# A hybrid decoder layer on one core: column sums of the adaLN projection shared otherwise between PE and DVE, a table's DMAs on another queue, and rows transposed before they are scaled

## The reference

```python
c_act = jax.nn.silu(c)
mod = c_act @ w_ada[l] + b_ada[l]
shift1, scale1, gate1, shift2, scale2, gate2 = jnp.split(mod, 6, axis=-1)

h = modulate(rms_norm(x, norm1_gain[l]), shift1, scale1)      # h * (1 + scale) + shift
proj = h @ w_in[l]
# ... attention with a relative position bias from rel_bias_table[t5_bucket(dist)],
# ... gated linear attention, and their gated merge
x = x + gate1[:, None, :] * (merged @ w_out[l])

h2 = modulate(rms_norm(x, norm2_gain[l]), shift2, scale2)
x = x + gate2[:, None, :] * conv_ffn(h2, w_ffn_up[l], ffn_conv_w[l], ffn_conv_b[l], w_ffn_down[l])
```

## Time and profile before

| | |
|---|---|
| median of 3 runs | 1686.44 us (1682.76 to 1691.81) |
| the profiled execution's own time | 1683.97 us |
| its span in the profile | 1681.8 us |
| PE, DVE, ACT busy | 96%, 71%, 49% of the span |
| PE's granted clock, mean | 0.972 |

### The profile page before, as it was taken

The page is one execution under the profiler, slowest core; times in us unless marked ns, Lnnn a source line. Parts: engine busy times, 40 slices in busy tenths (PEclk is TensorE's granted clock), DMA queues, the critical chain, the costliest instruction groups (busy, mean ns, idle before and its releaser), DMA issues.

```text
span 1681.8 us, 24152 instructions
## 1 busy us (share of the span) xinstructions
PE 1614.8 (96%) x8963; PEld 1400.2 (83%) x8963; DVE 1194.7 (71%) x1312; ACT 818.5 (49%) x971; POOL 30.4 (2%) x36
## 2 busy tenths in 40 slices
PE   4898889999999999999999799999999999999998
PEld 4777889998789988888888688888888888888887
DVE  5777735658877877988886667666666766789553
ACT  5344435346756653443444455555555555433332
POOL 0000000000002200000000000000000000000000
PEclk8888999999989999999999899999999999999999
DMA  7988877766756789998997366666666666799663
GB/s 284 346 294 304 296 178 258 265 233 200 260 166 213 226 281 341 354 342 323 335 329 255 101 189 190 186 194 188 188 188 190 191 190 188 279 376 348 203 206 114
DMA packets 195235, 411.72 MB, mean 245 GB/s; under 512 B 14754, under 2 KB 19406, under 8 KB 194654
## 3 DMA queue, kind: packets, MB, share of 16 engines
q1 hardware_dynamic: 195006, 410.53, 73.9%
q10 hardware_dynamic: 160, 0.26, 0.0%
HBM read 405.23 MB, written 5.25 MB: 244 GB/s over the span
## 4 chain that ended last, share of the span: by engine, by line
PE 91%; DVE 3%; ACT 2%; DMA 2%; issue 1%; SPq 0%; ACTq 0%; DVEq 0%
PE ps L1358 90%; DMA early<-in_w_ada 1%; DVE colacc L960 1%; DMA stage<-in_w_in 1%; ACT w_hi L601 1%; PE ps L1472 0%; PE ps L1583 0%; PE ps L1725 0%; ACT xnT L622 0%; DVE w_lo L907 0%; PE ps L1679 0%; DVE xr L1269 0%; DVE acc L918 0%; DVE xn L1259 0%; ACT p L772 0%
## 5 line engine op out<-in xcount | busy, mean ns | idle before, releaser
L601 ACT ACTIVATE w_hi<-stage 128x1024 fp32r<-128x1024 f32 x528 | 557.1, 1059 | 740.6 <-PE ps L1358 711.2
L907 DVE TENSOR_TENSOR w_lo<-stage,w_hi 128x1024 fp32r<-128x1024 f32 x528 | 648.9, 1231 | 378.0 <-ACT w_hi L601 376.1
L1358 PE MATMUL ps<-h,w_hi 128*128 128x512 f32 x1408 | 489.4, 394 | 0.0
L1358 PE MATMUL ps<-h,w_lo 128*128 128x256 f32 x1408 | 390.5, 277 | 0.0
L1358 PEld LDWEIGHTS ps<-h,w_hi 128*128 128x128 f32 x1408 | 264.7, 188 | 61.4
L1358 PEld LDWEIGHTS ps<-h,w_lo 128*128 128x128 f32 x1408 | 264.9, 188 | 0.0
L1358 PE MATMUL ps<-h_hi,w_hi 128*128 128x256 f32 x672 | 194.9, 290 | 0.0
L1358 PE MATMUL ps<-h_lo,w_hi 128*128 128x256 f32 x672 | 191.7, 285 | 0.0
L1358 PE MATMUL ps<-h_hi,w_lo 128*128 128x256 f32 x672 | 191.6, 285 | 0.0
L1358 PE MATMUL ps<-w_hi,h_hi 128*128 128x512 f32 (+1 forms) x416 | 170.1, 409 | 4.0 <-DVE w_lo L907 4.0
L1358 PE MATMUL ps<-w_hi,h_lo 128*128 128x512 f32 (+1 forms) x416 | 164.6, 396 | 0.0
(11 more groups left out here) (245 smaller groups left out, 1813.1 us busy)
## 6 DMA issues: line engine op xcount, KB each, us to landing
stage<-in_w_in SPq DMA_DIRECT2D x184, 512.0 KB, 4.0
stage<-in_w_ffn_up SPq DMA_DIRECT2D x176, 512.0 KB, 3.7
ada<-in_w_ada SPq DMA_DIRECT2D x96, 512.0 KB, 6.2
stage<-in_w_ffn_down SPq DMA_DIRECT2D x88, 512.0 KB, 4.8
early<-in_w_ada SPq DMA_DIRECT2D x64, 512.0 KB, 8.5
ada<-in_w_in SPq DMA_DIRECT2D x32, 512.0 KB, 4.8
stage<-in_w_branch_gla SPq DMA_DIRECT2D x32, 512.0 KB, 6.2
stage<-in_w_out SPq DMA_DIRECT2D x32, 512.0 KB, 5.8
```

Source lines behind the costliest of these rows:

```text
L601: act.activation(w_hi[:, u.slot(k)], stage[:, u.slot(k)], ACT.Copy).then_inc(hi_done, 1)
L907: TT(w_lo[:, u.slot(k)], stage[:, u.slot(k)], w_hi[:, u.slot(k)].bitcast(F32), ALU.subtract).then_inc(lo_done, 1)
L1358: return pe.matmul(out, lhsT, rhs, start=start, stop=stop, skip_group_check=True)
```

## The change

It has four parts.

1. **Column sums.** `PE_PARTS` says which parts of a quarter PE does itself: parts 0 and 1 in quarter 0, 6 and 7 in quarters 1 to 4, part 7 in quarters 5 to 7. DVE does the others. `reduce_early` is split: in quarter 0 its own matmuls stand before the transposes of x, and `sum_early(0)` behind them. PE's part counts in a semaphore `col_pe`, for which the reload of its buffers waits.
2. **DVE's order.** The low halves are turned by two units against the quarters: the last column instructions of quarter q now stand ahead of `lo(6q)`, where before they stood behind `lo(6q+2)`. SP's order of loads in a quarter is turned with them. PE's order of units and reductions is as before.
3. **The bias table.** Both DMAs are on ACT's queue: the write behind `hi(52)`, the read behind the heads' norms. SP loads unit 55 straight behind unit 54.
4. **The output projection.** PE transposes x1 unscaled, block by block: that of block b stands behind the fourth unit of block b+1, the last one behind the projection; ACT copies it to `x1T`. The last block is gated in two halves, one a token block, the first when half of the last unit is done. The row factor is formed by Sqrt and a reciprocal on DVE; it is put on the diagonal of `diag2`, and one matmul with `ones` spreads it over all partitions (`rs_b`, in PSUM). `h2_f` multiplies `x1T` by gain and `rs_b`; the shift goes in as ACT's bias and as DVE's scalar. `xn2` is gone.

```diff
-ON_DVE = 2 * (EARLY - 1)
+PE_PARTS = ((0, 1), (6, 7), (6, 7), (6, 7), (6, 7), (7,), (7,), (7,))
+DVE_PARTS = tuple(tuple(p for p in range(EARLY) if p not in mine) for mine in PE_PARTS)
...
                 if n >= EARLY:
-                    if part == EARLY - 1:
-                        sp.wait_ge(col_sum, quarter)
+                    before = DVE_PARTS[quarter - 1]
+                    if part in before:
+                        sp.wait_ge(col_done, COLS_BEFORE[quarter - 1] + 2 * (before.index(part) + 1))
                     else:
-                        sp.wait_ge(col_done, ON_DVE * (quarter - 1) + 2 * (part + 1))
+                        sp.wait_ge(col_pe, quarter)
...
-            for n in range(45, 55):
+            for n in range(45, 56):
                 load_first(n)
-            sp.wait_ge(rel_sb, 1)
-            sp.dma_start(rel_dram, rel_rows[:].unsqueeze(1).broadcast_to([HQ, P + 1, P])).then_inc(rel_out, 16)
-            load_first(55)
...
             for k in range(45, 55):
                 hi(u, k)
+                if k == 52:
+                    act.wait_ge(rel_sb, 1)
+                    act.dma_start(rel_dram, rel_rows[:].unsqueeze(1).broadcast_to([HQ, P + 1, P])).then_inc(rel_out, 16)
...
+            act.wait_ge(col_sum, 8)
+            act.wait_ge(col_done, COLS_BEFORE[8])
             act.wait_ge(rel_out, 16)
+            act.dma_start(bias[:], by_query).then_inc(bias_in, 16)
...
+            def x1_turned(b):
+                act.wait_ge(x1_tr, b + 1)
+                act.activation(x1T[:, 4 * b:4 * b + 4], ps[:, 1] if b == 3 else b56, ACT.Copy).then_inc(x1T_ready, 1)
...
-            rstd_of(rs2[:], rs2[:], D).then_inc(n2_rstd, 1)
+            act.activation(rs2[:], rs2[:], ACT.Sqrt, scale=1.0 / D, bias=eps[:, 0:1]).then_inc(n2_rstd, 1)
...
-                    f = TS(xr[:, kt % 4], ps[:, pair // 2 % 2, kt % 4], a2[:, kt:kt + 1], mod[:, 3 * KT + kt:3 * KT + kt + 1], ALU.mult, ALU.add)
+                    f = STT(out=xr[:, kt % 4], in0=x1T[:, kt], scalar=a2[:, kt:kt + 1], in1=rs_b, op0=ALU.mult, op1=ALU.mult)
...
+                for part in PE_PARTS[q]:
+                    pe.wait_ge(early_full[part], 16 * (q + 1))
                     for r in range(2):
-                        mm(b4[:, j:j + 1], early[:, EARLY - 1, r, j * P:(j + 1) * P], cact[:, ON_DVE + r:ON_DVE + r + 1], j == 0 and r == 0)
-                pe.wait_ge(col_done, (q + 1) * ON_DVE)
+                        kt = 2 * part + r
+                        for j in range(NT):
+                            f = mm(b4[:, j:j + 1], early[:, part, r, j * P:(j + 1) * P], cact[:, kt:kt + 1],
+                                   part == PE_PARTS[q][0] and r == 0 and j == 0)
+                f.then_inc(col_pe, 1)
+                if q:
+                    sum_early(q)
...
+            x1_turn(3)
+            pe.wait_ge(diag2_done, 1)
+            pe.wait_ge(ps_free[0], 16)
+            mm(rs_b, ones[:], diag2[:], True, True).then_inc(rs_row, 1)
```

More of the change, by code:

```diff
@@ L64 @@
 EARLY = 8
-ON_DVE = 2 * (EARLY - 1)
+PE_PARTS = ((0, 1), (6, 7), (6, 7), (6, 7), (6, 7), (7,), (7,), (7,))
+DVE_PARTS = tuple(tuple(p for p in range(EARLY) if p not in mine) for mine in PE_PARTS)
+COLS_BEFORE = tuple(2 * sum(len(p) for p in DVE_PARTS[:q]) for q in range(9))
 E_GATE1, E_GATE2 = 4, 8
@@ L227, in layer @@
     sq_junk = sb("sq_junk", 124, [P, NB])
-    xn2 = sb("xn2", 80, [P, 2, D])
+    x1T = sb("x1T", 48, [P, KT, T])
+    diag2 = sb("diag2", 108, [P, 2 * P])
     xr = sb("xr", 104, [P, NT, T])
@@ L854, in _ @@
                         square_sums(b - 1)
-            own(act.activation(eps[:, 1:2], eps[:, 0:1], ACT.Ln))
+                    if b and k == AHEAD + 5:
+                        x1_turned(b - 1)
+            own(act.activation(eps[:, 1:2], eps[:, 0:1], ACT.Sqrt))
             square_sums(3)
+            hi(Run(U_WOUT + 24), 7 + AHEAD)
             act.wait_ge(n2_sum, 1)
-            rstd_of(rs2[:], rs2[:], D).then_inc(n2_rstd, 1)
+            act.activation(rs2[:], rs2[:], ACT.Sqrt, scale=1.0 / D, bias=eps[:, 0:1]).then_inc(n2_rstd, 1)
             for pair in range(8):
+                if pair == 2:
+                    x1_turned(3)
                 act.wait_ge(h2f, pair + 1)
@@ L863, in _ @@
                     kt = 2 * pair + j
-                    f = act.activation(h2[:, kt, 0], xr[:, kt % 4], ACT.Copy)
+                    f = act.activation(h2[:, kt, 0], xr[:, kt % 4], ACT.Identity, bias=mod[:, 3 * KT + kt:3 * KT + kt + 1])
                 f.then_inc(h2hi_done, 1)
@@ L946, in _, with columns @@
             u = Run(0)
-            def columns(n):
-                quarter, part = n // 8, n % 8
-                dve.wait_ge(early_full[part], 16 * (quarter + 1))
+            def columns(q, index):
+                part = DVE_PARTS[q][index]
+                dve.wait_ge(early_full[part], 16 * (q + 1))
+                to = colacc[:, q % 2]
                 for r in range(2):
                     kt = 2 * part + r
-                    to = colacc[:, quarter % 2]
-                    if n or r:
-                        dve.wait_ge(col_done, ON_DVE * quarter + kt)
-                    if kt == 0:
-                        TS(to, early[:, part, r], cact[:, 0:1], None, ALU.mult).then_inc(col_done, 1)
+                    done = COLS_BEFORE[q] + 2 * index + r
+                    if done:
+                        dve.wait_ge(col_done, done)
+                    if index == 0 and r == 0:
+                        TS(to, early[:, part, r], cact[:, kt:kt + 1], None, ALU.mult).then_inc(col_done, 1)
                     else:
@@ L1012, in _ @@
                     take_shift(q - 4)
+            lo(u, 43)
+            h_of(6)
+            lo(u, 44)
+            h_of(7)
             dve.wait_ge(vec_tr, 5)
@@ L1455, in _ @@
             pe.transpose(b7[:, 0:P], vrows[:, 0, :], ident[:]).then_inc(vec_tr, 1)
+            pe.wait_ge(cact_ready, 1)
+            reduce_early(0)
             for t in range(2):
@@ L1703, in _, with x1_turn @@
                     spread_mod(3 + i, acc, (b4, b7))
+            def x1_turn(b):
+                pe.wait_ge(x1_done, b + 1)
+                if b == 0:
+                    pe.wait_ge(m_done, 4)
+                elif b < 3:
+                    pe.wait_ge(x1T_ready, b)
+                for j in range(NT):
+                    for t in range(2):
+                        cols = slice((NT * b + j) * P, (NT * b + j + 1) * P)
+                        f = pe.transpose((ps[:, 1] if b == 3 else b56)[:, j, t * P:(t + 1) * P], x1[:, t, cols], ident[:])
+                f.then_inc(x1_tr, 1)
             for b in range(4):
@@ L1711, in _ @@
                         pe.wait_ge(m_done, 4 if k >= 6 else k // 2 + 1)
-                    token_unit(u, k, ps_tok[:, par], m_hi, m_lo, k == 7)
+                    token_unit(u, k, ps_tok[:, par], m_hi, m_lo, k == 7, wout_half if b == 3 and k == 7 else None)
+                    if b and k == 3:
+                        x1_turn(b - 1)
                     if b == 0 and k == 1:
```

169 lines of the change are left out of this document (96 added, 73 removed).

## The result

The changed kernel takes 1661.06 us (median of 4 runs, 1655.2 to 1666.72) against 1685.29 us (4 runs, 1682.76 to 1691.81): a ratio of 0.9841, 95% interval 0.9801 to 0.9882. Run again beside other kernels it gave 1656.57 us, ratio 0.9837 (0.9791 to 0.9883). Its profiled execution took 1655.64 us (span 1653.7) where that of before took 1683.97 (1681.8): 28.3 us less.

The account below looks back on a forecast made before the run. PE bounds the kernel, its waits costing idle time and then low clock. Terms -8.7, 0, -4.5, -7.5 and -3 sum to -23.7 us: 1660.3 from the profiled 1683.97, plus 2.5 for the median, so 1663 us; range 1652 to 1677.

Parts of the forecast that it names:

- Start and quarter 1: Up to quarter 1's reduction: unit 0 starts 5.8 us earlier and loads gain more, -8.7 us.
- Quarters 2 to 4: Column sums there: PE's wait goes, but its second part and a clock fall once a quarter cancel that, 0 us.
- Quarters 5 to 7: Column sums there: waits of 2.2 and about 2 us can go, DVE nearly full; -4.5 us, between 0 and -9.
- DVE will be late now and then: In quarters 5 to 7, DVE's 19 us of work against PE's period of 19.2 to 20.2 us.
- Bias table: Stretch about the table: the wait for the heads' squares and the lower clock go, less costs; -7.5 us, between -8 and +4.
- a queue served in order: At the bias table: unit 55's load needed 14 us because it stood behind the write in one queue.
- Projection: Behind the output projection: first unit 7.1 us earlier, less 3.2 for transposes and 1 more; -3 us, between +1 and -5.
- The clock holds: Rival, quarters 2 to 7: PE's clock stays high through the column matmuls, some 3 us more in four quarters; 1651, chance 7%.
- The other queue doesn't help: Rival at the bias table: unit 55 lands no earlier, the term is 0; 1670, chance 12%.
- DVE or the loads are the bound: Rival in the quarters: only the start's 5.8 us and a third of the rest come; 1669, chance 15%.
- The write starves the loads: Rival at the bias table: each load in flight takes 14 us, PE stands up to 8 us more; 1678, chance 8%.
- The low clock that lasts through all six units: Rival in quarters 1 to 4: low clock through all six units, 14 us a quarter; 1720, chance 3%.

Follow-up runs that it names:

- One_part: The changed kernel with PE doing only part 7 itself in quarters 1 to 4 too, and DVE part 6; ratio to the kernel before 0.9767 (0.9725 to 0.9809).
- after_again: The changed kernel, unchanged, run and profiled once more beside other kernels; 1656.57 us, ratio to the kernel before 0.9837 (0.9791 to 0.9883).
- bias_only: The kernel before with only the bias table's write and read on ACT's queue and unit 55 loaded behind unit 54; ratio 0.9944 (0.9913 to 0.9974).
- proj_only: The kernel before with only the fourth part, x1 transposed unscaled in the output projection; ratio to the kernel before 0.9954 (0.9927 to 0.9981).

## Why the prediction was right, and where its sizes were off

The time came out 2 us from the forecast, 1661.06 against 1663, and that closeness is partly luck: the profiles moved by 28.1 and 26.4 us where 23.7 was forecast, and the medians mix executions of two lengths. The mechanisms held but for two steps, in quarters 5 to 7 and in what makes the table's move work.

**Start and quarter 1**, -8.7: -9.3. Unit 0 at 28.56 (28.3 foreseen), the reduction at 44.24 (44.8), and no wait for part 7: that the loads gain more than PE was right. Units 0 to 4 took 15.7 us, not 16.5: the low spell about unit 0 was 6.8 us long where before had 13.7.

**Quarters 2 to 4**, 0: +1.2 over the four periods from quarter 1's reduction to quarter 5's. The wait went and the clock fell once a quarter, as said. But the term was the net of two large ones: the turned order's gain, and PE's second part that took it back. One_part shows it, with periods of 20.7 to 21.2 us. The prediction took PE's second part and the order as one edit there, and so did not ask what the order would be worth without it.

**Quarters 5 to 7**, -4.5: -8.1. This is the step that was mis-sized. "DVE will be late now and then" failed: PE waits for `colacc` in none of them (in after_again once, 0.49 us), and DVE for PE instead. The arithmetic set 19 us of DVE against 19.2 to 20.2 of PE. It left out that PE's period has low clock in it: it was 21.1 and 21.5 us, as the prediction's own "some 22 us" for these quarters would have said. The low spell behind quarter 7's sum (1.7 us) went as well, but by luck: after_again has it, of 3.4 us, at 187.

**Bias table**, -7.5: -9.6 in the stretch, of which 1.7 are that low spell; -8.1 in after_again and -8.2 in bias_only, which have a spell there. The size was right. The reason relied on was not: the 14 us of unit 55 were taken for "a queue served in order", but the loads on the other queue stood behind the write nearly as long (up to 12.4 us). The Trainium skill (DMA: Bandwidth & Descriptors, Issuing engines are not separate DMA queues) says that DMAs run on the same 16 engines whichever engine started them, and with that the trace agrees (8.5 to 12.4 us for the loads). It also says that they interleave, and from 214 to 222 us they did not. The estimate of -0.7 us from its sentence on the issue time left out what the move does to the order: unit 55 ahead of the write, and the read no longer ahead of the next loads.

**Projection**, -3: -2.8 in after, -4.6 alone. The first unit stands 10.9 us behind the last of the projection (908.15 - 2.48 = 905.67 to 916.57), where 10.8 was worked out. Of the difference 1.7 us lie far ahead of the projection: about 100 us behind the head sum after has a longer low spell than before and proj_only (a mean clock of 0.95 against 0.97 over 100 us). No run ties this spell to a part of the change.

**The rivals.** "The clock holds" is out (0.50 behind the sums of quarters 1 to 6). "The other queue doesn't help" and "DVE or the loads are the bound" are out by bias_only and by PE's waits. "The write starves the loads" is half true: the loads took 8.5 to 12.4 us, but four slots and ACT's work on the norms cover that, and PE waits for none. The low clock that lasts through all six units is out too: the longest spell, in quarter 2 behind a wait of 1.00 us for `early`, was 10.2 us, where the others were 3.4 or 6.8.

## What to carry to other kernels

Where a step does two things at once (a wait hidden by more work, and an order that removes it), price each alone: here the order was worth it, and the extra work cost 6 us. Narrow matmuls did better in short pieces between wide ones (1.3 us over three quarters), if their operands have landed: moved ahead to a part that lands last they cost more than the clock gives. The large write in short rows held up the loads of the other queue too. So issue the load that is needed next ahead of it, and keep a DMA that must wait for it from standing ahead of other loads.

## What was not expected of the hardware

PE has two rates at a granted clock of 1.00 through the whole up projection, some 345 or 352 ns for a pair of matmuls, one per execution; its cause is open. A 1 MB write in rows of 512 bytes moved at 102 GB/s, and in bias_only at the same rate, and for 8 us the loads issued on the other queue moved nothing beside it. And the same code has low spells of other lengths from one execution to the next. Quarter 1's reduction begins within 1 us in after and after_again, but the spell behind it is 3.4 us long in the one and 6.8 in the other, and the head sums lie 1.5 us apart. So a difference of one or two us at a mark proves nothing by itself.
